# A two-layer decoder trunk on one core: 37 constant products ahead of the first adaLN products, and a scale product moved ahead of the last row transposes

## What is computed

```python
c_act = jax.nn.silu(c)
for i in range(DEPTH):
    mod = c_act @ ada_w[i] + ada_b[i]
    sh_m, sc_m, g_m, sh_f, sc_f, g_f = [m[:, None, :] for m in jnp.split(mod, 6, axis=-1)]
    h = rmsnorm(x, norm_mix_g[i]) * (1.0 + sc_m) + sh_m
    y = pool_mixer(h, ...) if i % N_MIXERS == 0 else moba_attention(h, ...)
    x = x + g_m * y
    h = rmsnorm(x, norm_ffn_g[i]) * (1.0 + sc_f) + sh_f
    x = x + g_f * hier_moe(h, ...)
return rmsnorm(x, final_norm_g)
```

## Time and profile before

| | us |
|---|---|
| median of 3 runs | 685.07 |
| lowest and highest of them | 684.03, 686.86 |
| the profiled execution, its time | 685.0 |
| its span, first to last instruction | 683.2 |
| around the span | 1.8 |
| TensorE busy | 629.4 (92%) |
| VectorE, ScalarE, GpSimd busy | 251.4, 120.2, 61.3 |
| weights and other reads | 271.59 MB, 399 GB/s over the span |
| mean granted TensorE clock | 0.985 |

### The profile page before, as it was taken

One profiled execution on the slowest core, in us unless ns is written; L12 is line 12 of the kernel. 1 busy time (PEld: TensorE's weight loads), 2 busy tenths in 40 slices (PEclk: granted clock), 3 DMA queues, 4 the chain that ended last, 5 costly groups with the idle time before them and its releaser, 6 DMA issues.

```text
span 683.2 us, 12930 instructions
## 1 busy us (share of the span) xinstructions
PE 629.4 (92%) x4790; PEld 385.5 (56%) x4790; DVE 251.4 (37%) x668; ACT 120.2 (18%) x312; POOL 61.3 (9%) x187
## 2 busy tenths in 40 slices
PE   4899899999889999999999999999999996798995
PEld 1455465555455455546888788877554442454542
DVE  0024423222222222234679497147523230232233
ACT  4013530000000000014144234138100000000003
POOL 7000011100101101000000000000111110000100
PEclk9999999999999999999999999999999997999999
DMA  9999999999999999999998989966999999999993
GB/s 352 419 420 423 425 425 431 430 423 430 437 429 426 435 425 428 428 417 420 419 421 333 358 342 425 426 272 270 345 425 421 427 426 422 424 425 425 423 421 129
DMA packets 27690, 273.32 MB, mean 400 GB/s; under 512 B 3188, under 2 KB 3700, under 8 KB 4984
## 3 DMA queue, kind: packets, MB, share of 16 engines
q1 hardware_dynamic: 27640, 272.65, 95.6%
HBM read 271.59 MB, written 1.05 MB: 399 GB/s over the span
## 4 chain that ended last, share of the span: by engine, by line
PE 84%; DMA 9%; issue 4%; DVE 1%; ACT 1%; SPq 1%; ACTq 0%; DVEq 0%
PE bank L845 74%; DMA ring<-in_ada_w_dram 9%; PE bank L1053 7%; PE bank L1263 2%; PE bank L1577 1%; SPq L507 0%; ACT hx L2089 0%; PE bank L1431 0%; PE bank L1438 0%; DVE ye L2130 0%; ACT reg_b L1895 0%; DVE ye L2127 0%; ACT reg_b L1707 0%; ACTq L178 0%; DVE xh L2396 0%
## 5 line engine op out<-in xcount | busy, mean ns | idle before, releaser
L845 PE MATMUL bank<-ring,xh 128*64 128x256 f32 (+2 forms) x2496 | 306.4, 428 | 29.3 <-issue 27.6
L845 PEld LDWEIGHTS bank<-ring,xh 128*64 128x64 f32 (+1 forms) x2496 | 171.1, 134 | 125.8 <-issue 70.5
L2127 DVE TENSOR_TENSOR reg_c<-reg_c,bank 128x128 f32<-128x128 f32 x58 | 16.7, 288 | 174.8 <-ACT reg_c L1783 96.5
L773 POOL COPY xh<-reg_a 128x256 f32 (+1 forms) x106 | 41.9, 406 | 405.1 <-PE bank L845 281.4
L845 PE MATMUL bank<-reg_b,ring 128*128 128x256 f32 x256 | 57.2, 380 | 0.4 <-ACT reg_b L1940 0.4
L1053 PE MATMUL bank<-ye,reg_b 32*128 32x512 f32 (+1 forms) x432 | 52.8, 599 | 0.0
L845 PEld LDWEIGHTS bank<-reg_b,ring 128*128 128x128 f32 x256 | 48.0, 190 | 7.1 <-issue 0.9
L2127 DVE TENSOR_TENSOR ye<-bank,reg_c 128x512 f32<-128x512 f32 (+1 forms) x60 | 40.1, 670 | 29.7 <-PE bank L845 29.7
L2396 DVE COPY xh<-bank 128x128 f32<-128x128 f32 x58 | 16.6, 286 | 92.9 <-PE bank L845 92.9
L845 PE MATMUL bank<-ring,cact 128*32 128x512 f32 (+1 forms) x320 | 35.5, 555 | 14.5 <-DMA ring<-in_ada_w_dram 14.4
L1783 ACT ACTIVATE reg_c<-bank 128x128 f32<-128x128 f32 x32 | 8.9, 278 | 204.0 <-PE bank L845 204.0
(11 more groups left out here) (211 smaller groups left out, 458.2 us busy)
## 6 DMA issues: line engine op xcount, KB each, us to landing
ring<-in_exp_w_dram SPq DMA_DIRECT2D x38, 2048.0 KB, 20.2
ring<-in_exp_w_dram SPq DMA_DIRECT2D x20, 3072.0 KB, 16.0
ring<-in_exp_w_dram SPq DMA_DIRECT2D x50, 1024.0 KB, 18.7
ring<-in_ada_w_dram SPq DMA_DIRECT2D x48, 1024.0 KB, 17.2
ring<-in_w_qkv_dram SPq DMA_DIRECT2D x12, 1024.0 KB, 16.6
ring<-in_w_o_dram SPq DMA_DIRECT2D x4, 1024.0 KB, 8.2
gu_spare<-in_exp_w_dram SPq DMA_DIRECT2D x1, 2048.0 KB, 20.6
hx<-in_exp_w_dram SPq DMA_DIRECT2D x2, 1024.0 KB, 19.7
```

The source lines that it names most:

```text
L773: nc.gpsimd.tensor_copy(xe[:, b, k0:k1, t * CAP:(t + 1) * CAP], hS[:, k0:k1, bass.ds(off, CAP)])\
L845: return nc.tensor.matmul(o_, l_, r_, start=start, stop=stop)
L2127: return nc.vector.tensor_tensor(o_, a_, b_, op)
```

## The change

TensorE's program gets, ahead of its first instruction, a wait for `filled` at 1 and 37 products of `ones` (128 by 128) on the first 64 columns of `ones`, into `bank[6]`, whose result nobody reads. In layer 2, `third(9, 0, 3)` moves from behind `turn_rows(3)` to ahead of it.

```diff
@@ -1340,6 +1340,9 @@
                     overflow(L)
                     last_rows(L)
 
+            pe.wait_ge(S("filled"), 1)
+            for _ in range(37):
+                mm(bank[6][:, 0:64], ones[:, :], ones[:, 0:64], True, True)
             pe.wait_ge(S("cact_ready"), 1)
             for i in range(3):
                 third(0, i, 0)
@@ -1492,8 +1495,8 @@
             turn_rows(1)
             pe.wait_ge(S("xr_dve"), 2)
             turn_rows(2)
+            third(9, 0, 3)
             turn_rows(3)
-            third(9, 0, 3)
             pe.wait_ge(S("x_rows"), 4)
             raw_turned(0)
             columns(3)
```

## The result

The changed kernel takes 692.41 us (691.59 to 693.92, 4 runs) against 684.66 (684.03 to 686.86, 4 runs): ratio 1.0108, 95% interval 1.0093 to 1.0124. The profiled execution took 692.49 us, its span is 690.8, 7.6 us more than before. The forecast was 685.0, in a range of 683.2 to 686.6.

What follows compares the result with a forecast made beforehand. The weight stream was taken to bound up to some 334 us, TensorE up to some 500, the stream again afterwards. 685.0 - 0 (products) - 0.1 (order) = 684.9, given as 685.0, range 683.2 to 686.6.

Steps and rivals of the forecast that it cites:

- Value of part one: 0, with bounds of 0 and, for the slow end, 0 too: The 37 products at TensorE's start change the total by 0, as idle time at landings absorbs a few us.
- The price of a product: At the start, 0.24 us each at full clock, 0.50 at the lower clock; 11.7 us for all 37.
- my slow bound of 18.5: At the start, all 37 products at the lower clock take 18.5 us and end at 19.6.
- The clock at 21.66: From 21.66 us the clock falls as before; staying at full clock would gain up to 2.0 us there.
- this lateness: At the start, later first thirds and `ada(3)` issue, at 14.6 to 16.1 us, cost nothing given 17 us of queue.
- the point near 30 us where the stream runs dry: Transfers issued ahead of `ada(3)` last to about 30 us; its issue may come 12 us later without a gap.
- Part two: In layer 2, the moved scale product starts `columns(3)` 0.15 us earlier; -0.1 at the end, bounds -0.15 and +0.4.
- Rival B: In layer 2, the moved product stands before its landing and TensorE idles: +0.4, 685.4 us; chance 0.15.
- Rival A: From 21.66 to 51.06 us, TensorE's saved time comes back: 683.0, at most 680.8 us; chance 0.10.
- Rival C: At the start, the products end beyond 30 us and the stream runs dry: at 35 us, +5, 690; chance 0.02.
- The range: Whole kernel: 683.2 to 686.6 us, from the early-time rival's 683.0 and the spread of the runs.
- a 93% chance of "same": Whole kernel: chance 0.93 of no measurable change, about 0.5% or 3.4 us; faster 0.04, slower 0.03.

Runs made afterwards that it cites:

- e5: The changed kernel with 27 very small products (108 instructions) added behind the 37, 256 instructions more than the kernel before: 685.82 us, ratio 1.0024.
- e4: The changed kernel with 108 waiting no-operations added ahead of the 37 products, 256 instructions more than the kernel before: 693.09 us, ratio 1.0119.
- e2: The changed kernel without the 37 products, so only `third(9, 0, 3)` is moved against the kernel before: 684.55 us, ratio 0.9999.
- e6: The changed kernel with 15 products instead of 37, 60 instructions more than the kernel before: 685.57 us, ratio 1.0021.
- e7: The changed kernel with 28 products instead of 37, 112 instructions more than the kernel before: 691.01 us, ratio 1.0103.
- e11: The kernel before with 64 very small products (256 instructions) at its head, old order: 685.87 us, ratio 1.0011.
- e12: 37 very small products placed behind the jump, after layer 2's third adaLN third, none at the head: 690.79 us, ratio 1.0076 against the kernel before.
- e10: The kernel before with 50 very small products (200 instructions) at its head, old order: 688.21 us, ratio 1.0053.
- e1: The changed kernel with `third(9, 0, 3)` put back behind `turn_rows(3)`, so only the 37 products are new: 692.64 us, ratio 1.0105.
- e3: The kernel before with 148 waiting no-operations ahead of its first product, no new products, old order: 693.27 us, ratio 1.0123.
- e9: The kernel before with 37 very small products (148 instructions) at its head, old order: 691.48 us, ratio 1.0116.
- e8: The changed kernel with 41 products instead of 37, 164 instructions more than the kernel before: 693.66 us, ratio 1.0130.

## Why the prediction was wrong, point by point

- **The step that failed** is the sum's "Value of part one: 0, with bounds of 0 and, for the slow end, 0 too". It priced the 37 products by what they do and when they end. What cost 7.7 us was their 148 instructions of code, at a place 300 us later. So the cost was put at nothing, and the runs showed in its place a stall of 4.32 us where TensorE ran out of code, about 3.1 us of lower clock behind it, and 0.78 us ahead of it whose cause stays open; 7.6 us of this reach the end. I named no such rival; the queue of packets called "instruction" stood on the page and I didn't read it.
- **The price of a product** was mis-sized. 37 took 16.0 us (1.12 to 17.10), 0.43 each, where I took 11.7 us for all; that is near my slow bound of 18.5. The column of the granted clock says 1.00 there, as before, but their pace is the same from first to last, and the clock rose only within the three thirds behind them, which took 3.87 us together against the 3.2 I expected. During their own 16 us these products didn't raise the clock.
- **The clock at 21.66** was read wrongly. I expected it to fall as before, since the idle stretches ahead of 19.19 and 21.66 would remain in part. They were gone: the thirds of `ada(1)` ran end to end, 24 matrix instructions from 22.80 in 2.78 us, and the band sums took 1.56 us instead of 2.23. At 73 us no more than 0.15 us of it was left.
- **That this lateness costs nothing** was right: `ada(3)` was issued at 21.08 instead of 15.27, the first product at 73 us is unmoved, and e5 bears 19.9 us at the start. The point near 30 us where the stream runs dry was right too (e4: the issue at 32.52 left 67 GB/s); the price of running dry was too low, 2.5 us by the rival's rule against 6.9.
- **Part two** gives 0.17 us up to `first_rows`, and 334.50 at `shift_sums` against 334.49: mechanism right, but nothing of the -0.1 can be seen at `shift_sums`, and the medians can't tell 0.1 us. Rival B did not occur: (9,0) started at 317.08 with no wait for a landing in e2; in e4, where the stream was late, it waited 0.60 us.
- **Rival A** (TensorE's early time comes back) is out: at 73 us only 0.15 us came back (73.10 against 73.25). **Rival C** did not occur in the change.
- **The range** was made of costs that I knew of; with a jump over 218 instructions in the program, an edit of 148 instructions ahead of it had no business with a 93% chance of "same".

## What to carry to other kernels

Instructions added anywhere ahead of a jump move every border of the code behind it. Before such an edit, look where the timeline has jumps, and whether TensorE works 5 to 6 us in the piece of code it lands in, which is what the next piece took here. If an edit that should be free isn't, fill it up with very small products to a whole piece of 256 instructions, as in e5: if the time comes back, it was the borders. Here an idle stretch <-issue inside a run of products that share one wait was missing code, and the lower clock behind it cost about 3 us more. An idle stretch <-issue between two runs isn't proof: the chain of the kernel before has one of 5.67 us at 562.77, and the last instruction packet ahead of it starts at 551.2, the next at 572.1.

## What was unexpected of the hardware

The next piece of code seems to be asked for when a piece is entered, not earlier: in the changed kernel no packet of the queue falls in 151 to 296 us, while TensorE is in its loop, and still it lacked a piece two borders on. The times of the packets fit. Where the jump itself enters a piece (before, e2, e4, e5, e6, e7, e11, e12), the packet starts 2.3 to 2.6 us after it. In e10, where TensorE ran into the piece some 3 us ahead of the jump, it starts at 311.2, ahead of the jump at 311.9. In all kernels that stall there, TensorE goes on 2.3 to 2.7 us after the packet's start. The rule in the section of the Trainium skill cited above, on a taken branch out of the window, doesn't cover this: in the changed kernel the landing place was, by the count, in the piece already there, and the stall came at the border behind it.

An instruction packet may also cost the weight stream. Up to 300 us, the queue of instructions in the kernel before and in the changed one:

```profile
q8 instruction: 8, 0.13, 0.2%
```

```profile
q8 instruction: 9, 0.15, 0.2%
```

The profiled kernels with 8 (before, e2, e6, e12) begin layer 2 at 310.7 to 311.1 us, those with 9 at 311.6 to 312.1 where no stall stands at the jump itself (after, e1, e3, e5, e7, e9, e11). But the ninth packet comes at two places. In e5, e10 and e11, whose programs are 200 or 256 instructions longer, it is there by 180 us, and near the end of layer 1's loop they are late: the run of 40 matrix instructions that starts at 285.93 in the kernel before starts at 287.10 to 287.33. This would account for the 1.2 to 1.3 us that e5 and e11 keep. In the changed kernel, e1, e3, e7, e8 and e9 it comes at 296.7 to 297.4. Up to there they are level with the kernel before (285.8 to 286.0), and their 0.8 us or so arise at 301, in an idle stretch <-issue of 0.8 to 1.3 us that the other kernels don't have. In e9 a packet stands between 16 and 20 us where the kernel before has none, and the third that started at 19.19 started at 20.35; that lateness is gone by 286 us. All this is correlation; no run changed the number of packets alone.
